# Two-block transformer on one core: three quarters of the first block's output projection as fp32r parts

## The reference

```python
x = x + jnp.concatenate([out_a, out_b, out_m], axis=-1) @ w_out[l]
x = x + conv_ffn(rms_norm(x, ffn_norm_g[l]), w_up[l], conv_w[l], conv_b[l], w_down[l])
```

## Time and profile before

| | us |
|---|---|
| median of 3 runs | 1062.64 (1062.47 to 1063.32) |
| the profiled execution | 1063.16, of which its span is 1061.4 |
| TensorE busy | 911.6 (86% of the span) |
| VectorE / ScalarE / GpSimd busy | 551.6 / 358.2 / 76.0 |
| mean granted TensorE clock | 0.944 |

### The profile page before, as it was taken

The page is one execution under the profiler, slowest core; times in us unless marked ns, Lnnn a source line. Parts: engine busy times, 40 slices in busy tenths (PEclk is TensorE's granted clock), DMA queues, the critical chain, the costliest instruction groups (busy, mean ns, idle before and its releaser), DMA issues.

```text
span 1061.4 us, 19424 instructions
## 1 busy us (share of the span) xinstructions
PE 911.6 (86%) x8462; PEld 706.2 (67%) x8462; DVE 551.6 (52%) x1020; ACT 358.2 (34%) x698; POOL 76.0 (7%) x113
## 2 busy tenths in 40 slices
PE   9999999999999999999999998667655666657784
PEld 8787777489999888988989965334333343334442
DVE  4775688858888766798867643211112121211211
ACT  5710355246776536456553341000001010000002
POOL 3022710000000000331010000000000000000000
PEclk9999999999999999999999999988888887989878
DMA  9545453695554565876549899999999999999994
GB/s 350 164 165 185 143 190 120 219 286 170 160 174 174 202 233 190 267 233 215 179 148 387 350 386 426 430 427 430 426 431 427 429 428 429 430 427 429 426 431 200
DMA packets 76715, 316.21 MB, mean 298 GB/s; under 512 B 4087, under 2 KB 28064, under 8 KB 64208
## 3 DMA queue, kind: packets, MB, share of 16 engines
q1 hardware_dynamic: 71972, 302.24, 72.5%
q0 software_dynamic: 4512, 12.62, 4.0%
q10 hardware_dynamic: 140, 0.04, 0.0%
HBM read 311.72 MB, written 1.06 MB: 295 GB/s over the span
## 4 chain that ended last, share of the span: by engine, by line
PE 61%; DMA 25%; DVE 7%; ACT 3%; issue 3%; ACTq 0%; SPq 0%; POOL 0%; DVEq 0%
PE ps L486 59%; DMA w<-in_w_up 18%; DMA w<-in_w_down 4%; DMA w<-in_w_gate 3%; DVE sp L1940 1%; DMA rot<-q 1%; PE ps L612 1%; PE ps L2803 1%; DVE acc L1003 0%; ACT hts L2937 0%; DVE wr L680 0%; DVE w L1041 0%; ACTq L3200 0%; ACT sp L1931 0%; DVE q L2314 0%
## 5 line engine op out<-in xcount | busy, mean ns | idle before, releaser
L486 PE MATMUL ps<-w,xg 128*32 128x256 f32 x2016 | 156.5, 469 | 96.7 <-DMA w<-in_w_up 75.8
L486 PE MATMUL ps<-hb,sp 128*128 128x256 f32 x1824 | 224.4, 283 | 0.0
L486 PEld LDWEIGHTS ps<-hb,sp 128*128 128x128 f32 x1824 | 218.6, 188 | 3.0 <-issue 2.5
L486 PEld LDWEIGHTS ps<-w,xg 128*32 128x32 f32 x2016 | 83.3, 130 | 167.5 <-issue 143.6
L1940 DVE TENSOR_TENSOR sp<-w,sp 128x1024 fp32r<-128x1024 f32 x122 | 144.6, 1220 | 37.5 <-ACT sp L1931 37.4
L1931 ACT ACTIVATE sp<-w 128x1024 fp32r<-128x1024 f32 x122 | 122.3, 1052 | 46.0 <-PE ps L486 42.4
L3013 DVE TENSOR_TENSOR cst<-ps,cst 64x256 f32<-64x256 f32 x31 | 13.3, 428 | 214.6 <-ACT cst L2924 214.6
L2924 ACT ACTIVATE cst<-ps 64x256 f32<-64x256 f32 x31 | 11.7, 377 | 309.8 <-PE ps L486 309.8
L3039 DVE TENSOR_TENSOR ost<-ps,cst 32x256 f32<-32x256 f32 x120 | 50.5, 420 | 103.3 <-PE ps L486 100.5
L486 PE MATMUL ps<-w,hts 128*32 128x256 f32 x1024 | 63.6, 390 | 13.1 <-ACT hts L2937 10.3
L486 PE MATMUL ps<-sp,ab 128*128 128x512 f32 x264 | 61.7, 395 | 0.0
(11 more groups left out here) (430 smaller groups left out, 1304.7 us busy)
## 6 DMA issues: line engine op xcount, KB each, us to landing
w<-in_w_down SPq DMA_DIRECT2D x36, 2048.0 KB, 35.8
w<-in_w_gate SPq DMA_DIRECT2D x32, 2048.0 KB, 28.1
w<-in_w_up SPq DMA_DIRECT2D x31, 2048.0 KB, 33.1
w<-in_w_in SPq DMA_DIRECT2D x13, 2048.0 KB, 9.5
w<-in_w_up SPq DMA_DIRECT2D x22, 1024.0 KB, 7.6
w<-in_w_ada SPq DMA_DIRECT2D x8, 2048.0 KB, 8.7
w<-in_w_out SPq DMA_DIRECT2D x4, 2048.0 KB, 8.0
w<-in_w_ada POOLq DMA_DIRECT2D x8, 768.0 KB, 5.8
```

The source lines that it names most:

```text
L486: return q.eng.matmul(o, l, r, start=start, stop=stop, skip_group_check=True)
```

## The change

Three quarters are made with fp32r parts, and one stays f32 and goes first. The order is (0,1) in f32, then (0,0), (1,0) and (1,1) with `mm3`. GpSimd makes hi and lo of the weights of c = 0 (`wout0_gp`, 8 copies and 8 subtractions of 128x512) as soon as the recurrence has left the buffers. For c = 1 ScalarE makes hi (`wout1_sc`, 4 copies of 128x1024) and GpSimd lo (`wout1_gp`, 8 subtractions); lo is written over the f32 weights, so that it waits for the first quarter. ScalarE and VectorE split `cat` (`cat_sc`, `cat_ve`, one 128x1024 instruction each per half). The transposes of h = 0 move from between quarters 3 and 4 into the middle of quarter 4. The second split of the up projection moves behind the norm of h = 1 on ScalarE and VectorE. The split buffers change places (`SP_AT`), and with them slots 3 and 4 in the experts' order. The counters `r_i`, `r_zf` and `u_z` become one, `gp_fill`.

```diff
@@ sizes and places @@
+        SP_AT = (4096, 0, 8192)
+        sp_r = [[sb(f"sp{i}{z}", RB + SP_AT[i] + 2048 * z, 2048, R) for z in range(2)] for i in range(3)]
+        wo_hi0, wo_hi0_7, wo_hi1 = sb("woh0", RB + 4608, 3584, R), sb("woh07", 29088, 512, R), sb("woh1", RB, 4096, R)
+        cat_hi, cat_lo = sb("cath", 49312, 2048, R), sb("catl", 44592, 2048, R)
@@ expert slots 3 and 4 change places @@
-        EXS = (6, 8, 0, 7, 2, 1, 4, 5, 3, 9)
+        EXS = (6, 8, 0, 7, 2, 1, 3, 5, 4, 9)
...
-                    q.wait_ge(s["o2_mm"], {4: 2, 5: 3, 3: 5}[ch.slot_no])
+                    q.wait_ge(s["o2_mm"], {3: 2, 5: 3, 4: 5}[ch.slot_no])
@@ the output projection @@
-        def wout_pe(q, h):
...
-            for c in range(2):
...
-                for k in range(8):
-                    t = mm(q, psum[b], catv[:, k, 128 * h:128 * h + 128], w[:, k, :], k == 0, k == 7)
...
+        WO = [(0, 1), (0, 0), (1, 0), (1, 1)]
...
+        def wout0_gp(q):
+            e, raw = q.eng, wo_raw(0)
+            q.wait_ge(*chunks["out", 0].tok)
+            q.wait_ge(s["r_mm"], RN["u6", 1])
+            q.wait_ge(s["gp_fill"], 12)
+            for n in range(4):
+                for k in (2 * n, 2 * n + 1):
+                    e.tensor_copy(wo_hi(0, k), raw[:, k, :]).then_inc(s["wo_hi"], 1)
+                for k in (2 * n, 2 * n + 1):
+                    q.wait_ge(s["wo_hi"], k + 1)
+                    e.tensor_tensor(wo_low(0)[:, k, :], raw[:, k, :], wo_hi(0, k).bitcast(F), SUB).then_inc(s["wo_lo"], 1)
+
+        def wout1_gp(q):
+            e, raw = q.eng, wo_raw(1)
+            q.wait_ge(s["wo_mm"], 1)
+            for k in range(8):
+                q.wait_ge(s["nhi"], 15 + k // 2)
+                e.tensor_tensor(wo_low(1)[:, k, :], raw[:, k, :], wo_hi(1, k).bitcast(F), SUB).then_inc(s["wo_lo"], 1)
+
+        def wout1_sc(q):
+            q.wait_ge(*chunks["out", 1].tok)
+            q.wait_ge(s["r_mm"], RN["y", 1])
+            for n in range(4):
+                ks = slice(2 * n, 2 * n + 2)
+                q.eng.activation(v(wo_hi1, 8)[:, ks, :], wo_raw(1)[:, ks, :], ACT.Copy).then_inc(s["nhi"], 1)
...
+        def cat_sc(q, h):
+            q.wait_ge(s["a1_c"], NA)
+            q.wait_ge(s["r_n"], 4 * h + 4)
+            q.wait_ge(s["r_mm"], RN["y", 1])
+            q.eng.activation(cat_half(cat_hi, h), cat_half(cat, h), ACT.Copy).then_inc(s["nhi"], 1)
+
+        def cat_ve(q, h):
+            q.wait_ge(s["nhi"], 13 + h)
+            q.eng.tensor_tensor(cat_half(cat_lo, h), cat_half(cat, h), cat_half(cat_hi, h).bitcast(F), SUB).then_inc(s["nlo"], 1)
+
+        def wout_pe(q, n):
+            h, c = WO[n]
+            b = 2 * h + c
+            if n == 0:
                 q.wait_ge(s["a1_c"], NA)
+                q.wait_ge(s["r_n"], 4)
+                q.wait_ge(*chunks["out", 1].tok)
+            else:
+                q.wait_ge(s["nlo"], 13 + h)
+            take(q, b)
+            for k in range(8):
+                o = slice(128 * h, 128 * h + 128)
+                if n == 0:
+                    t = mm(q, psum[b], catv[:, k, o], wo_raw(1)[:, k, :], k == 0, k == 7)
+                else:
+                    q.wait_ge(s["wo_lo"], 8 * c + k + 1)
+                    t = mm3(q, psum[b], [v(a, 8)[:, k, o] for a in (cat_hi, cat_lo)], [wo_hi(c, k), wo_low(c)[:, k, :]], k == 0, k == 7)
+                if k == 3:
+                    yield
...
@@ split_sc: what the first two splits of the up projection wait for @@
-            q.wait_ge(*(half_done(j - 3) if j > 2 else (s["npe"], 12) if j == 2 else (s["r_n"], 8)))
+            q.wait_ge(*(half_done(j - 3) if j > 2 else (s["npe"], 12) if j == 2 else (s["wo_mm"], 3 + j)))
@@ ScalarE @@
             weave(rwkv_sc(q), beside_sc(q))
+            cat_sc(q, 0)
+            cat_sc(q, 1)
+            wout1_sc(q)
...
-            split_sc(q, 1)
             later_squares_sc(q, 2, x, [(s["x1"], 3), (s["x1"], 4)], psum_all[:, 2048:3072])
             later_root_sc(q, 2)
+            split_sc(q, 1)
@@ VectorE @@
             weave(rwkv_ve(q), beside_ve(q, first))
+            cat_ve(q, 0)
+            cat_ve(q, 1)
             for i in (6, 7):
                 for _ in ada_ve(q, i):
                     pass
-                wout_ve(q, 0, (i - 6,))
+                wout_ve(q, i - 6)
...
@@ GpSimd @@
             rwkv_gp(q)
+            wout0_gp(q)
+            wout1_gp(q)
@@ TensorE @@
-            for n, _ in enumerate(wout_pe(q, 1)):
-                if n == 1:
+            for _ in wout_pe(q, 1):
+                pass
+            for _ in wout_pe(q, 2):
+                pass
+            for n, _ in enumerate(wout_pe(q, 3)):
+                if n == 0:
                     feat_pe(q, 2, xn1, ft2, hs=(0,))
```

More of the change, by code:

```diff
@@ L96 @@
         "r_z", "r_mm", "in_a", "r_l2", "r_lo", "r_kk", "r_kp", "r_L", "r_E", "r_AR", "r_bs", "r_T", "r_bt",
-        "r_m", "r_d", "r_of", "r_t", "r_u", "r_i", "r_zf", "r_rhs", "r_sa", "r_st", "r_ys",
-        "r_ya", "r_yv", "r_n", "wo_mm", "x1",
-        "hi", "split", "half_mm", "u_z", "u_ev", "u_c", "u_v", "u_s", "a_hi", "a_lo", "dn_mm", "x_ffn", "q_ev", "rot0", "rot1", "rope",
+        "r_m", "r_d", "r_of", "r_t", "r_u", "gp_fill", "r_rhs", "r_sa", "r_st", "r_ys",
+        "r_ya", "r_yv", "r_n", "wo_hi", "wo_lo", "wo_mm", "x1",
+        "hi", "split", "half_mm", "u_ev", "u_c", "u_v", "u_s", "a_hi", "a_lo", "dn_mm", "x_ffn", "q_ev", "rot0", "rot1", "rope",
         "od_sq", "mg_mm", "mg_v", "mg_hi", "mg_lo", "od_mm", "od_n", "od_hi", "od_lo", "o2_mm", "x_mix",
@@ L243, in block_kernel @@
         xn1 = sb("xn1", RB + 8192, 2048)
-        sp_r = [[sb(f"sp{i}{z}", RB + 4096 * i + 2048 * z, 2048, R) for z in range(2)] for i in range(3)]
+        SP_AT = (4096, 0, 8192)
+        sp_r = [[sb(f"sp{i}{z}", RB + SP_AT[i] + 2048 * z, 2048, R) for z in range(2)] for i in range(3)]
+        wo_hi0, wo_hi0_7, wo_hi1 = sb("woh0", RB + 4608, 3584, R), sb("woh07", 29088, 512, R), sb("woh1", RB, 4096, R)
+        cat_hi, cat_lo = sb("cath", 49312, 2048, R), sb("catl", 44592, 2048, R)
         hb = [sb(f"hb{z}", P1 + 2048 * z, 2048, R) for z in range(2)]
@@ L374, in block_kernel @@
         NVEC = 6
-        FIRST_PARTS = 12
+        FIRST_HI, FIRST_LO = 18, 14
         def ada_done(i):
@@ L1586, in rwkv_pe @@
             yield
-            q.wait_ge(s["r_zf"], 4)
+            q.wait_ge(s["gp_fill"], 12)
             q.wait_ge(s["r_u"], 11)
@@ L1796, in rwkv_ve @@
             yield
-        def wout_pe(q, h):
-            if h == 0:
-                q.wait_ge(s["a1_c"], NA)
-            q.wait_ge(s["r_n"], 4 * h + 4)
-            for c in range(2):
-                w = v(chunks["out", c].ap, 8)
-                q.wait_ge(*chunks["out", c].tok)
-                b = 2 * h + c
-                take(q, b)
-                for k in range(8):
-                    t = mm(q, psum[b], catv[:, k, 128 * h:128 * h + 128], w[:, k, :], k == 0, k == 7)
-                    if k % 4 == 3 and k < 7:
-                        yield
-                t.then_inc(s["wo_mm"], 1)
-                free[b] = [(s["x1"], b + 1)]
-                yield
@@ L1816, in wout_ve, with wo_raw, wo_hi @@
-        def wout_ve(q, h, cs=(0, 1)):
-            for c in cs:
-                o = x[:, h, 512 * c:512 * c + 512]
-                q.wait_ge(s["wo_mm"], 2 * h + c + 1)
-                q.eng.tensor_tensor(o, psum[2 * h + c], o, ADD).then_inc(s["x1"], 1)
+        WO = [(0, 1), (0, 0), (1, 0), (1, 1)]
+        def wo_raw(c):
+            return v(chunks["out", c].ap, 8)
+        def wo_hi(c, k):
+            if c == 0 and k == 7:
+                return wo_hi0_7
+            return (v(wo_hi1, 8) if c else v(wo_hi0, 7))[:, k, :]
@@ new lines, in wo_low @@
+        def wo_low(c):
+            return v(slotr[chunks["out", c].slot_no], 8)
+        def wout0_gp(q):
+            e, raw = q.eng, wo_raw(0)
+            q.wait_ge(*chunks["out", 0].tok)
+            q.wait_ge(s["r_mm"], RN["u6", 1])
+            q.wait_ge(s["gp_fill"], 12)
+            for n in range(4):
[4 more added lines that the diff above has]
+                    e.tensor_tensor(wo_low(0)[:, k, :], raw[:, k, :], wo_hi(0, k).bitcast(F), SUB).then_inc(s["wo_lo"], 1)
@@ new lines, in cat_half @@
+        def cat_half(a, h):
+            return v(a, 8)[:, :, 128 * h:128 * h + 128]
+        def cat_sc(q, h):
[6 more added lines that the diff above has]
+            q.eng.tensor_tensor(cat_half(cat_lo, h), cat_half(cat, h), cat_half(cat_hi, h).bitcast(F), SUB).then_inc(s["nlo"], 1)
@@ new lines, in wout_pe @@
+        def wout_pe(q, n):
+            h, c = WO[n]
+            b = 2 * h + c
+            if n == 0:
+                q.wait_ge(s["a1_c"], NA)
+                q.wait_ge(s["r_n"], 4)
[12 more added lines that the diff above has]
+                    yield
+            t.then_inc(s["wo_mm"], 1)
+            free[b] = [(s["x1"], n + 1)]
+            yield
@@ L1823, in beside_pe, with wout_ve @@
+        def wout_ve(q, n):
+            h, c = WO[n]
```

(5 more changed lines are left out.)

31 lines of the change are left out of this document (16 added, 15 removed).

## The result

| | median of 5 runs, us | range |
|---|---|---|
| before | 1062.63 | 1062.43 to 1063.32 |
| after | 1078.84 | 1078.16 to 1080.91 |

The ratio is 1.0148, 95% interval 1.0131 to 1.0165: 16.2 us slower, where 9.5 were forecast. The direction was right; the size is outside the range (1060 to 1078).

A forecast was written before the change was run, and what follows sets the result against it. The prediction took TensorE to end the output projection last, VectorE next with almost no slack, and weight-bound experts to pass shifts on. It summed -3.3 + 5.5 + 7.3 = +9.5 us to 1072.2 us, range 1060 to 1078.

The forecast's parts named there:

- TensorE's saving: Output projection: fp32r products at 0.233 us save TensorE 4.0 us; with VectorE ending last, the gain is 3.3 us.
- The state 5.5 us late: Beside the recurrence: ten VectorE instructions take turns with GpSimd's first job, delaying the state 5.5 us (bounds 2.7 to 9.9).
- rival 3: Beside the recurrence: GpSimd's copy to fp32r takes 1.28 us instead of 0.69, adding 3 us, to 1075.2 us; chance 13%.
- Behind line 1781 GpSimd's remaining work falls into VectorE's waits for the recurrence, and adds nothing.: After the recurrence's state: GpSimd's leftover work costs nothing, so the output projection starts just 5.5 us later.
- the later wait: Last quarter of the output projection: TensorE waits 6 us for scaled rows; a falling clock there adds up to 1 us.
- The second stretch: Output projection: eight VectorE instructions take turns with GpSimd's subtractions for c = 1, costing 7.3 us (bounds 5.4 to 7.3).
- The last addition ended by VectorE: End of the output projection: VectorE, not TensorE, finishes last, at 221.1 us; TensorE finishes at 219.3.
- From the up projection to the end: Behind the output projection: the up projection starts 9.5 us later and the distance to the end stays the same.
- Rival 4: In the experts: their transfers set the end and absorb the delay; time within 0.2% of 1062.6 us; chance 5%.
- rivals 1 and 2: Turns cost nothing on the path, 1059.3 us, chance 15%; or only the output projection's turns cost, 1066.6 us, chance 12%.

The follow-up runs named there:

- e2_only_writes: The changed kernel with each of GpSimd's 24 instructions replaced by two memsets that read nothing, so the weights' parts are zero: 1060.49 us, ratio 0.9963.
- e8_state_late: The kernel before with eight additions on VectorE ahead of the recurrence's state, GpSimd idle: 1073.29 us, ratio 1.0082.
- e9_late_kept: The kernel before with eight VectorE additions ahead of the recurrence's state and 11 unused TensorE products in its wait for that state: 1068.00 us, ratio 1.0046.
- e3_no_second: The changed kernel without GpSimd's 8 subtractions for c = 1; the last quarter multiplies hi in place of lo: 1071.01 us, ratio 1.0073.
- e7_no_first: The changed kernel without GpSimd's hi and lo for c = 0; those quarters multiply hi of c = 1 instead: 1067.74 us, ratio 1.0034.
- e6_both: The changed kernel with GpSimd's first job waiting for the recurrence's state and VectorE's modulation chunk 7 moved behind the second split: 1066.36 us, ratio 1.0010.

## Why the prediction was off, by its own steps

- **TensorE's saving.** Right: products of `cath` are 0.233 us apart where the clock is full, and GpSimd left out, the last addition comes 3.5 us earlier (3.3 forecast; e2_only_writes).
- **The state 5.5 us late.** Right in sum (5.4), with luck in its parts. The seven large instructions cost 3.3 us more instead of 4.7 (the four of line 1006 0.52 each, one weighting 0.83, the other nothing, the scaling 0.35), and the three on 128x2 cost 2.7 instead of 1.3; the two errors cancel. The cast takes 0.90 us on average (not 0.69, nor rival 3's 1.28). Rival 3 falls.
- **"Behind line 1781 GpSimd's remaining work falls into VectorE's waits for the recurrence, and adds nothing. The whole of the output projection starts 5.5 us later."** The first of these sentences held on TensorE's way; the step to the second failed. The output projection starts 12.5 us later on the trace's clock, 13.9 counted from the mark ahead of the new work. The late state makes TensorE stand for 4.6 us, the granted clock falls from 2.4 to 1.2 GHz at 174.9 us, and the tail of the recurrence, which TensorE bounds, costs 8.5 us more. The pair e8_state_late and e9_late_kept shows that such a wait does this by itself, and the equal timelines of after and e8_state_late that it was so in after. The prediction allowed for the clock only in the later wait, "up to 1 us", and had not asked how long TensorE would stand at the state. That wait could be read from its own numbers: the state 5.5 us late, with TensorE at the clock 1.00 and 8.20 of 8.2 us busy up to there, means a wait of about 5.
- **The second stretch, 7.3 us.** Near: 6.8 by e3_no_second, 6.5 by e7_no_first against e2_only_writes. GpSimd's subtractions took 1.68 us against the 1.70 that the sum used. From the first quarter to the last addition after is 4.2 us longer (9.0 - 4.8), against 4.0 forecast, but that this fits so well is chance: -3.5 + 6.5 are 3.0, and the other 1.2 are the low clock in the last quarter, the next term.
- **The last addition ended by VectorE.** Wrong by 1.2 us (9.9 from the second addition against 8.6 in e7_no_first), in the direction that was allowed for: TensorE waited 5.21 us, its clock fell, and VectorE stood ready 1.1 us before the last quarter was done.
- **From the up projection to the end.** As forecast, within the scatter: 1.0 us shorter, where this distance lies between 837.0 and 842.5 us in the fourteen profiled executions. Rival 4 falls, rivals 1 and 2 as well: the turns cost in both stretches, and of a state 4.8 us late the recurrence hid 0.4 with the clock held (e9_late_kept).

In numbers: 5.4 + 8.5 - 3.5 + 6.5, and 1.2 for the last quarter, is 18.1; less the 1.4 us ahead of the new work and the 1.0 at the end, 15.7, as the two spans differ. The sum of 9.5 lacked a single large term, 8.5 us, nearly as large as itself. That the time misses it by only 6.7 is in part owed to 2.4 us that lie outside the stage.

## What to carry to other kernels

When a step makes TensorE wait some us in a stretch where it sets the pace, don't count the wait alone: look for the granted clock behind it, and price the stretch that follows by the time at the low level (here 0.35 us for each us). Where such a wait can't be removed, products that nobody reads can hold the clock: in the two runs that tried it they did where they filled the wait, and not where 1.15 us were left. And count work for an idle GpSimd by what it reads: beside a full VectorE, one subtraction of 128x512 cost VectorE 0.67 to 0.85 us, so that saving TensorE 4 us with 16 subtractions was a bad trade where it was put, and at best an even one (e6_both).
